# GpSimd adds five of the embedding stage's squares to the running sum

## What is computed

```python
def rms_norm(x, gain, eps=EPS):
    xf = x.astype(jnp.float32)
    y = xf * lax.rsqrt(jnp.mean(xf * xf, axis=-1, keepdims=True) + eps)
    return (y * gain.astype(jnp.float32)).astype(x.dtype)
...
        x = x + rms_norm(mixed, post_norm_gain[i])
        e = rms_norm(p[i] @ w_ple_proj[i], ple_norm_gain[i])
        x = x + jax.nn.sigmoid(x @ w_ple_gate[i]) * e
...
def fourier_mixer(h, w_o):
    B, S, D = h.shape
    hg = h.astype(jnp.float32).reshape(B, S, FOURIER_GROUPS, FOURIER_GROUP_DIM)
    f = jnp.fft.fftn(hg, axes=(1, 3), norm="ortho").real.astype(h.dtype)
    return f.reshape(B, S, D) @ w_o
...
        h = modulate(rmsnorm(x, norm_mix_g[i]), sh1, sc1)
        m = fourier_mixer(h, w_fourier_out[j])
```

## Time and profile before

| | us |
|---|---|
| median of three runs | 1551.31 |
| lowest, highest | 1550.65, 1551.39 |
| the profiled execution, its own time | 1551.43 |
| span in its profile | 1549.3 |
| PE busy | 1534.8 |
| GpSimd busy | 866.8 |
| VectorE busy | 796.4 |
| ScalarE busy | 599.1 |

### The profile page before, as it was taken

The page is one execution under the profiler, slowest core; times in us unless marked ns, Lnnn a source line. Parts: engine busy times, 40 slices in busy tenths (PEclk is TensorE's granted clock), DMA queues, the critical chain, the costliest instruction groups (busy, mean ns, idle before and its releaser), DMA issues.

```text
span 1549.3 us, 21277 instructions
## 1 busy us (share of the span) xinstructions
PE 1534.8 (99%) x7254; PEld 1273.8 (82%) x7254; DVE 796.4 (51%) x1127; ACT 599.1 (39%) x886; POOL 866.8 (56%) x1040
## 2 busy tenths in 40 slices
PE   9999999999999999999999999999999999999997
PEld 7777888887988888888888888888889888888886
DVE  6887887887645544551545424446257454011113
ACT  7444444684522212223444334244345322122223
POOL 6445547657567765775463635535535766555551
PEclk9999999999999999999999999999999999999999
DMA  6534455234255554542232322313212553222221
GB/s 231 191 129 156 169 211 190 89 130 163 96 203 183 207 194 177 203 150 95 96 107 67 109 82 80 101 48 107 95 54 82 202 205 119 99 95 95 95 82 55
DMA packets 58233, 202.97 MB, mean 131 GB/s; under 512 B 6464, under 2 KB 8512, under 8 KB 58176
## 3 DMA queue, kind: packets, MB, share of 16 engines
q1 hardware_dynamic: 56880, 198.87, 37.4%
q10 hardware_dynamic: 1296, 3.30, 0.6%
HBM read 200.05 MB, written 2.10 MB: 130 GB/s over the span
## 4 chain that ended last, share of the span: by engine, by line
PE 76%; POOL 12%; issue 11%; DMA 0%; DVE 0%; ACT 0%; SPq 0%; POOLq 0%; DVEq 0%; ACTq 0%
PE banks L1723 20%; PE banks L1727 20%; PE banks L1726 20%; POOL w_lo L412 12%; PE banks L2228 2%; PE banks L2227 2%; PE banks L2224 2%; PE banks L1739 1%; PE banks L1742 1%; PE banks L1743 1%; PE banks L2264 1%; PE banks L2263 1%; PE banks L2262 1%; PE banks L2251 0%; PE banks L2250 0%
## 5 line engine op out<-in xcount | busy, mean ns | idle before, releaser
L412 POOL TENSOR_TENSOR w_lo<-w_raw,w_hi 128x256 fp32r<-128x256 f32 x1028 | 859.9, 869 | 647.1 <-ACT w_hi L444 647.0
L444 ACT ACTIVATE w_hi<-w_raw 128x1024 fp32r<-128x1024 f32 x257 | 270.2, 1057 | 645.7 <-PE banks L1723 586.9
L1723 PE MATMUL banks<-a_hi,w_lo 128*128 128x512 f32 x1228 | 482.1, 393 | 0.1
L1727 PE MATMUL banks<-a_hi,w_hi 128*128 128x512 f32 x1228 | 478.2, 389 | 0.0
L1726 PE MATMUL banks<-a_lo,w_hi 128*128 128x512 f32 x1228 | 478.1, 389 | 0.0
L1723 PEld LDWEIGHTS banks<-a_hi,w_lo 128*128 128x128 f32 x1228 | 230.8, 188 | 48.2 <-issue 0.8
L1727 PEld LDWEIGHTS banks<-a_hi,w_hi 128*128 128x128 f32 x1228 | 230.5, 188 | 48.3
L1726 PEld LDWEIGHTS banks<-a_lo,w_hi 128*128 128x128 f32 x1228 | 230.6, 188 | 47.0 <-issue 0.2
L1723 PE MATMUL banks<-b_hi,w_lo 128*128 128x512 f32 x572 | 223.7, 391 | 2.0 <-POOL w_lo L412 2.0
L1727 PE MATMUL banks<-b_hi,w_hi 128*128 128x512 f32 x572 | 222.6, 389 | 0.0
L1726 PE MATMUL banks<-b_lo,w_hi 128*128 128x512 f32 x572 | 222.6, 389 | 0.0
(11 more groups left out here) (289 smaller groups left out, 1638.7 us busy)
## 6 DMA issues: line engine op xcount, KB each, us to landing
w_raw<-in_W SPq DMA_DIRECT2D x258, 512.0 KB, 3.5
ada_raw<-in_ADA SPq DMA_DIRECT2D x112, 512.0 KB, 4.3
X<-in_XT SPq DMA_DIRECT2D x8, 256.0 KB, 6.9
scr<-in_DECAY ACTq DMA_DIRECT2D x4, 448.0 KB, 4.2
out<-X SPq DMA_DIRECT2D x4, 256.0 KB, 2.7
w_raw<-in_W SPq DMA_DIRECT2D x2, 256.0 KB, 3.8
scr<-in_PT ACTq DMA_DIRECT2D x1, 512.0 KB, 4.7
scr<-in_ROPE ACTq DMA_DIRECT2D x1, 512.0 KB, 4.4
```

Source lines behind the costliest of these rows:

```text
L412: pool.tensor_tensor(w_lo[:, c % RING, part], w_raw[:, c % RING, part], w_hi[:, c % RING, part].bitcast(fp32), ALU.subtract).then_inc(wlo, 1)
L444: act.activation(w_hi[:, c % RING, :], w_raw[:, c % RING, :], ACT.Copy).then_inc(whi, 1)
L1723: mm = pe.matmul(out, lo, x_hi, start=first, stop=False)
L1727: mm = pe.matmul(out, hi, x_hi, start=False, stop=last)
```

## The change

The squares of tiles 1 to 5 (`ON_POOL` is 5) are no longer written to the gate's banks but to the tiles of `E`, which are free by then, and GpSimd adds them to `sqsum`, under a new count `gate_sum`. GpSimd's program, a loop over the chunks before, now is: the low parts up to the gate's last chunk in a loop; the adds 1 and 2; the low part of chunk 50, add 3, that of chunk 51, add 4, that of chunk 52, add 5; then the rest in a second loop. VectorE keeps the adds of squares 6 and 7, and waits before add 6 for all five of GpSimd's. The bank of a gate tile 1 to 5 is given back by ScalarE's identity (L686), on which VectorE's low part then waits in place of the count `xh`.

```diff
--- before.py
+++ after.py
@@ -37,6 +37,7 @@
 N_ADA = 14
 ADA_RING = 2
 ADA_LAG = 6
+ON_POOL = 5
 
 
 COL = {}
@@ -274,7 +275,7 @@
         rot, rot_hi, rot_ready, v_mean, vv_hi, v_ready, gg_t, pd, pd_hi, y_sq, y_qs, y_r, y_f, y_hi, y_ready = (
             sem(n) for n in ("rot", "rot_hi", "rot_ready", "v_mean", "vv_hi", "v_ready", "gg_t", "pd", "pd_hi",
                              "y_sq", "y_qs", "y_r", "y_f", "y_hi", "y_ready"))
-        out_done = sem("out_done")
+        out_done, gate_sum = sem("out_done"), sem("gate_sum")
 
         block = ctx.enter_context(nc.Block())
         def key_rows(buf):
@@ -421,13 +422,29 @@
                                        ALU.subtract).then_inc(wlo, 1)
             for c in range(2, 4):
                 lo_part(flat, c)
-            n = N_CHUNK // 4
-            with pool.Fori(0, n - 1) as i:
-                at = At(i, chunk=4)
-                for s in range(4):
-                    lo_part(at, 4 + s)
-            for c in range(4 * n, N_CHUNK):
-                lo_part(flat, c)
+            def lo_parts(c, end):
+                n = (end - c) // 4
+                with pool.Fori(0, n) as i:
+                    at = At(i, chunk=4)
+                    for s in range(4):
+                        lo_part(at, c + s)
+                for c in range(c + 4 * n, end):
+                    lo_part(flat, c)
+
+            def add_gate_square(m):
+                pool.wait_ge(sq_ready, 8 * 3 + m + 1)
+                if m > 1:
+                    pool.wait_ge(gate_sum, m - 1)
+                pool.tensor_tensor(sqsum[:, :], sqsum[:, :], E[:, m, :], ALU.add).then_inc(gate_sum, 1)
+
+            c0 = CH["gate"]
+            lo_parts(4, c0 + 8)
+            add_gate_square(1)
+            add_gate_square(2)
+            for m in range(3, ON_POOL + 1):
+                lo_part(flat, c0 + m + 5)
+                add_gate_square(m)
+            lo_parts(c0 + ON_POOL + 6, N_CHUNK)
 
 
         @block.scalar
@@ -681,14 +698,14 @@
 
             def gate_post(m):
                 act.wait_ge(x_new, KD + m + 1)
-                dst = banks[:, BANK[t0 + m], :] if m else sqsum[:, :]
+                dst = sqsum[:, :] if m == 0 else E[:, m, :] if m <= ON_POOL else banks[:, BANK[t0 + m], :]
                 act.activation(dst, X[:, m, :], ACT.Square).then_inc(sq_ready, 1)
                 ins = act.activation(XH[:, m, :], X[:, m, :], ACT.Identity, bias=zero,
                                      scale=gs[:, KD + m:KD + m + 1])
-                if m:
+                if m > ON_POOL:
                     ins.then_inc(xh, 1)
                 else:
-                    read_out(ins, t0)
+                    read_out(ins, t0 + m)
 
             for n in range(8):
                 if n not in (3, 7):
@@ -1351,17 +1368,19 @@
                                      op1=ALU.subtract).then_inc(shift_ready, 1)
 
             def xg_low(m):
-                if m:
-                    dve.wait_ge(xh, m)
+                if m > ON_POOL:
+                    dve.wait_ge(xh, m - ON_POOL)
                 else:
-                    wait_read(dve, flat, t0)
+                    wait_read(dve, flat, t0 + m)
                 dve.scalar_tensor_tensor(out=XL[:, m, :], in0=X[:, m, :], scalar=gs[:, KD + m:KD + m + 1],
                                          in1=XH[:, m, :].bitcast(fp32), op0=ALU.mult,
                                          op1=ALU.subtract).then_inc(xl, 1)
 
             def add_gate_square(m):
                 dve.wait_ge(sq_ready, 8 * 3 + m + 1)
-                if m > 1:
+                if m == ON_POOL + 1:
+                    dve.wait_ge(gate_sum, ON_POOL)
+                else:
                     wait_read(dve, flat, t0 + m - 1)
                 read_out(dve.tensor_tensor(sqsum[:, :], sqsum[:, :], banks[:, BANK[t0 + m], :], ALU.add), t0 + m)
 
@@ -1371,7 +1390,7 @@
                 dve.wait_ge(e_ready, m + 1)
                 link(dve.scalar_tensor_tensor(out=bank, in0=bank, scalar=1.0, in1=E[:, m, :], op0=ALU.add, op1=ALU.mult))
                 dve.tensor_tensor(X[:, m, :], X[:, m, :], bank, ALU.add).then_inc(x_new, 1)
-                if m > 1:
+                if m > ON_POOL + 1:
                     add_gate_square(m - 1)
                 if m:
                     xg_low(m - 1)
```

## The result

The changed kernel takes 1556.58 us (median of 6 runs, 1555.30 to 1558.45), before 1551.35 us; the ratio is 1.0036, with a 95% interval of 1.0026 to 1.0046. So it is 5.2 us slower. The profiled execution took 1557.94 us for a span of 1556.2, 6.9 us more than the span of before, and its mean granted clock is 0.994.

A forecast was written before the change was run, and what follows sets the result against it. TensorE, busy 99% of the span, bounds the kernel. Median 1551.31 us plus 3.1 (3.0 for GpSimd's lateness, with the 1.17 gain never seen, and 0.1 for small meetings) gives 1554.4 us; range 1553.0 to 1557.0.

The forecast's parts named there:

- The bound and the event to follow: TensorE, 99% busy, bounds; its DFT 1 tile 5 is released at 326.19 by VectorE's add of square 6.
- Gain on VectorE: Gate stage: five adds leave VectorE, 3.0 us of issue time; TensorE's last quarter could come 1.17 us earlier.
- An add on GpSimd: One 128x512 add in GpSimd's queue was taken to cost 1.30 us.
- GpSimd's sum: GpSimd's queue up to add 5: 314.44 + 8.40 + 3 x 1.30 + 1.63 = 328.37; add 6 starts at 328.45, not 325.45.
- Everything behind it shifts by that; nothing else is late: From add 6 through DFT 1's statistics and last quarter, the whole stage is 3.0 us late.
- Low parts, loads, the split loop cost nothing: DFT 2's low parts end 2.7 and 2.3 us later, loads up to 2.7, all covered; the cut loop is hidden.
- The clock: Rival: TensorE's clock falls to 1.2 GHz in a 4 us gap before DFT 1's tile 5; 1556.6 us, chance 0.22.
- The likeliest case: Whole kernel: the forecast as worked out, 1554.4 us, within 1553.9 to 1555.0; chance 0.60.
- Given back later: Rival: TensorE's later stalls behind low parts shrink by up to 2.0 us; 1552.4 us; chance 0.13, including no difference.
- Faster: Rival: add 5 is done by about 324.4, so VectorE's relief reaches TensorE; 1.17 us gained, 1550.1 us, chance 0.05.

The follow-up runs named there:

- kernel with the other order: Changed kernel with GpSimd's adds 3 to 5 made ahead of DFT 2's low parts: 1549.78 us against 1551.12; again 1549.82 us against 1551.33.
- the kernel whose adds nobody waits for: Kernel before with the changed kernel's GpSimd program, its five adds going to a spare tile, VectorE keeping its seven: 1551.70 us against 1551.12.
- the kernel that keeps TensorE busy: Changed kernel plus 14 unused matmuls of 512 columns ahead of DFT 1's tile 5: 1554.43 us against 1551.12 for the kernel before.

## Why the prediction was right, and where not

- *The bound and the event to follow* (right). PE's idle time before tile 5 of DFT 1 is where the loss is, released by VectorE's add of square 6.
- *Gain on VectorE* (right, 1.02 us for 1.17). The kernel with the other order shows it, and there VectorE waits for ScalarE's tanh 0.18, 0.33 and 0.60 us, so ScalarE's pace limits it. In the changed kernel ScalarE's table load starts at 323.91, 16.10 us into the stage, against 17.18 before: 1.08 us earlier, where the prediction had 1.0.
- *An add on GpSimd: 1.30 us, from the half-width row and the memset* (right: 1.27 to 1.31 where nothing is met). The Trainium skill's "GPSIMD Engine Reference", section 3.1, led to an estimate of 1.25 to 1.27, slightly under the rows.
- *GpSimd's sum* (right within 0.3 us). Forecast for the start of add 6: 3.00 us late; measured 2.72 in the frame. From 315.11 to 328.72 are 13.61 us, of which 8.40 are low parts and 3.8 adds; 1.4 are left for the meetings, where 1.63 were assumed.
- *Everything behind it shifts by that; nothing else is late* (right: 2.98 us at the statistics and 3.08 at DFT 2 with the clock held, for 3.0). The small wait for VectorE's last low part, 0.18 us, was costed at 0.1.
- *Low parts, loads, the split loop cost nothing* (right, by the kernel whose adds nobody waits for). What was missed there is that GpSimd, busy without a pause, is in front of VectorE's low parts more often: 1.0 us of the stage, hidden here.
- *The clock* (wrong in its chance; its price near in size, but counted over too short a stretch). This is the step that failed: "No row here shows one, so none decides", and a chance of 0.22. The gap came out at 3.49 us, and ten of the eleven executions show a mean clock below the 0.998 of before. The price was put at 1.44 + 0.8 = 2.2 us, for what lies between the release and the last quarter of DFT 1. The profiles give 1.9 and 3.5 us at DFT 2, the medians 2.2 and 0.8 us (1556.58 and 1555.22 against 1554.43). In the first profile only 1.3 of the 3.5 us had arisen by the last quarter; the rest came behind it, where the products still ran at 1.2 GHz and the sum had no term. The likeliest case, 1554.4 us with a chance of 0.60, is the time of the kernel that keeps TensorE busy; the changed kernel took the rival's time, 1556.6. The range held because it had been drawn wide enough for this rival, and that the first median meets the rival's sum to the tenth is luck: the second is 4.5 us above before, between the two cases. A fall of the clock stood among the prediction's own signs of being wrong. The Trainium skill, "TensorE: Matmul & The Clock Gate", section "Why this matters for your kernels", had counted such gaps among those that put the array back to half rate; the trace agrees (3.49 us, then 0.50), and that case deserved the greater chance.
- *Given back later* (wrong as a mechanism). The long stall in the earlier trace rows was one execution's; a second profile of before, taken ahead of the forecast, would have cast doubt on it.
- *Faster* (fell). It needed add 5 done by 324.4, and the kernel with the other order shows that the condition was stated rightly: there it is done, and the gain is there.

## What to carry to other kernels

When work is moved to an engine with time to spare, ask for its place in that engine's queue and who waits for it: GpSimd had 44% of its time free, and the move still cost 5 us, because the wait was behind work that nobody wanted yet. Putting the urgent piece first gained in the stage nearly what the move could gain. Where a change opens a gap on TensorE like those seen here (with 2.3 us the mean clock was lower in five of ten executions, with 3.5 us in ten of eleven), add the price of its clock to that of the gap, and look at the granted clock of the stretch behind it.

## What the runs showed of the hardware

- TensorE's granted clock fell from 1.00 to 0.50 in or just behind an idle gap of 3.5 us in both profiles of the changed kernel, and stayed low for some 7 and 12 us of continuous work; a product of 256 columns then takes 0.21 us from start to start in place of 0.12. After gaps of 1.62 and 2.28 us it stayed at 1.00 in the one profiled execution of each; with the latter, five of ten executions have a lower mean clock.
- GpSimd and VectorE exclude each other for whole operations when VectorE has two inputs in SBUF: the second waits until the first is through. In the kernel before, one of VectorE's seven later low parts took 1.28 us in place of 0.75 and four of GpSimd's twelve operations 1.19 to 1.23 us in place of 0.74; with the spare adds, four of VectorE's took 1.19 to 1.29. VectorE's operations with one input in a PSUM bank (L1372, L1373, L1366) took 0.68 or 0.69 us throughout that stage.
